# Prompt attention: score groups of rows and columns alternate in one run, values follow in two blocks; f32r masks; preparation in the sample stage

## What is computed

```python
q_r = rope(q, fpos)                       # 16 heads of 64, 4 groups of keys and values
k_s, v_s = rope(kv[:, :, 2], fpos), kv[:, :, 3]
k_w, v_w = rope(kv[:, :, 4], fpos), kv[:, :, 5]
s_c = einsum('bqgrd,bngd->bqgrn', q_b, ck) * scale      # compressed blocks
p_c = masked_softmax(s_c, (c_end[None, :] <= qp[:, None])[None, :, None, None, :])
o_c = einsum('bqgrn,bngd->bqgrd', p_c, cv)
p_s = masked_softmax(s_s, m_s)            # selected branch; o_s = p_s v_s
p_w = masked_softmax(s_w, m_w)            # window branch;   o_w = p_w v_w
return g_b[..., 0:1] * o_c + g_b[..., 1:2] * o_s + g_b[..., 2:3] * o_w
```

## Time and profile before

| | |
|---|---|
| median of 3 runs | 2354.88 us (2352.86 to 2372.43) |
| profiled execution | 2356.08 us, its span 2354.3 us |
| mean granted clock of TensorE | 0.838 |
| busy: PE, DVE, ACT, POOL | 2059.4, 924.4, 610.2, 133.2 us (87, 39, 26, 6% of the span) |

### The profile page before, as it was taken

How to read it: one execution, slowest core, us unless ns; L and a number is a source line. 1 busy time by engine, 2 the same in 40 slices (tenths; PEclk the granted TensorE clock), 3 DMA queues, 4 the chain that set the end, 5 groups by cost and what they waited for, 6 DMA issues and landing times.

```text
span 2354.3 us, 33541 instructions
## 1 busy us (share of the span) xinstructions
PE 2059.4 (87%) x13375; PEld 1838.6 (78%) x13375; DVE 924.4 (39%) x1372; ACT 610.2 (26%) x847; POOL 133.2 (6%) x171
## 2 busy tenths in 40 slices
PE   3999676999999696997687779999998699999968
PEld 3777375999999696996574447777788699999958
DVE  4687745433334644114011122322333634343363
ACT  4222144322312223221101111222123423232223
POOL 0000003000000000004000021011100200000000
PEclk8999797999999898996666655555589799999979
DMA  4211013322222121213221200000003122222211
GB/s 131 59 36 36 18 54 118 97 83 89 89 89 89 36 77 53 72 54 92 55 62 46 72 0 1 1 1 1 1 1 99 36 90 87 91 82 79 89 36 56
DMA packets 149763, 138.82 MB, mean 59 GB/s; under 512 B 22674, under 2 KB 146914, under 8 KB 149471
## 3 DMA queue, kind: packets, MB, share of 16 engines
q1 hardware_dynamic: 148175, 129.94, 17.8%
q0 software_dynamic: 1504, 7.74, 1.0%
HBM read 130.79 MB, written 10.87 MB: 60 GB/s over the span
## 4 chain that ended last, share of the span: by engine, by line
PE 82%; DVE 9%; issue 2%; ACT 2%; SPq 1%; POOL 1%; DMA 0%; ACTq 0%; DVEq 0%; POOLq 0%
PE ps L360 47%; PE ps L1209 5%; PE ps L439 3%; PE ps L1182 3%; PE ps L399 3%; PE ps L1180 2%; PE ps L1196 2%; PE ps L1194 2%; PE ps L913 1%; DVE sub_out L1899 1%; PE ps L1052 1%; PE ps L739 1%; PE ps L738 1%; PE ps L740 1%; DVE rstd L466 1%
## 5 line engine op out<-in xcount | busy, mean ns | idle before, releaser
L360 PE MATMUL ps<-x_hi,w_hi 128*128 128x272 f32 x1920 | 409.4, 295 | 75.7 <-DVE x_lo L481 33.9
L360 PE MATMUL ps<-x_hi,w_lo 128*128 128x272 f32 x1920 | 404.1, 293 | 0.0
L360 PE MATMUL ps<-x_lo,w_hi 128*128 128x272 f32 x1920 | 403.2, 292 | 0.0
L360 PEld LDWEIGHTS ps<-x_hi,w_hi 128*128 128x128 f32 x1920 | 308.4, 193 | 84.4 <-issue 47.8
L345 DVE TENSOR_TENSOR w_lo<-w_raw,w_hi 128x2048 fp32r<-128x2048 f32 x102 | 233.6, 2293 | 250.1 <-ACT w_hi L340 249.1
L360 PEld LDWEIGHTS ps<-x_lo,w_hi 128*128 128x128 f32 x1920 | 309.3, 193 | 0.0
L360 PEld LDWEIGHTS ps<-x_hi,w_lo 128*128 128x128 f32 x1920 | 307.0, 193 | 0.0
L340 ACT ACTIVATE w_hi<-w_raw 128x2048 fp32r<-128x2048 f32 x102 | 194.5, 1907 | 296.5 <-PE ps L360 287.6
L360 PE MATMUL ps<-hid_hi,w_lo 128*128 128x272 f32 x1024 | 212.0, 288 | 0.0
L360 PE MATMUL ps<-hid_hi,w_hi 128*128 128x272 f32 x1024 | 211.6, 288 | 0.0
L360 PE MATMUL ps<-hid_lo,w_hi 128*128 128x272 f32 x1024 | 211.1, 288 | 0.0
(11 more groups left out here) (339 smaller groups left out, 2838.9 us busy)
## 6 DMA issues: line engine op xcount, KB each, us to landing
w_raw<-in_ffn_w_in SPq DMA_DIRECT2D x64, 512.0 KB, 4.6
w_raw<-in_ffn_w_out SPq DMA_DIRECT2D x64, 512.0 KB, 4.3
w_raw<-in_nsa_w_in SPq DMA_DIRECT2D x20, 512.0 KB, 4.3
w_raw<-in_conv_w_in SPq DMA_DIRECT2D x16, 512.0 KB, 5.5
w_raw<-in_ple_w_gate SPq DMA_DIRECT2D x16, 512.0 KB, 4.2
w_raw<-in_conv_w_out SPq DMA_DIRECT2D x8, 512.0 KB, 4.4
w_raw<-in_nsa_w_o SPq DMA_DIRECT2D x8, 512.0 KB, 4.6
x_tok<-in_x_prompt SPq DMA_DIRECT2D x4, 512.0 KB, 8.1
```

The costliest lines, as they stand in the source:

```text
L360: m = pe.matmul(o_, w[par][:, wcols:wcols + P], x[:, k, c_], start=f, stop=l)
```

## The change

- TensorE's order: in step i (now -1 to 15) the row groups of head i+1 and the column groups of head i alternate, j by j, in one run. Then come `out_rows` and the compressed parts, the ten values of head i for the selected branch, `shift(i+1)`, `cmp_out`, and the ten values of head i for the window branch. Values thus belong to head i and no longer to head i-1, and pT has one buffer instead of two. ScalarE and VectorE follow the new order.
- In each tile the low multiply comes second and the mask last. The mask is made of f32r copies of identity and mask (IDR, CAUR).
- The row form's low multiply takes 68 partitions instead of 64; GpSimd sets QB's four to zero ahead of each head's row scores.
- The preparation for the first group and the first two queries is moved into the sample stage: ScalarE's ahead of its sample work, GpSimd's (`prompt_prep`) behind it. v_one and the two f32r masks lie over a part of kv_tok, so GpSimd waits for the stores of kv_tok ahead of them.

The diff, cut to its core:

```diff
-        (PT,), e = over(xt_at, ("pT", [P, 2, 5, SEQ], F32))
+        (PT,), e = over(xt_at, ("pT", [P, 5, SEQ], F32))
...
+        (VX, IDR, CAUR), e = over(kv_at, ("v_one", [P, 2, 2, QT, HD + 1], F32), ("ident_r", [P, P], F32R),
+                                  ("causal_r", [P, P], F32R))
...
+        def keys_high(act, L, g):
+            if g >= 2:
+                act.wait_ge(S["t_full"], 5 * GQ * (g - 1))
+            for br in range(2):
+                L(act.activation(KA[g % 2][0:HD, br, :], KT[:, br, g, :], ACT.Copy), S["k_hi"], wait=False)
+
+        def q_high(act, L, i):
+            if i >= 3:
+                act.wait_ge(S["t_full"], 5 * (i - 2))
+            rows = slice(i % 2 * HD, i % 2 * HD + HD)
+            L(act.activation(QA[i % 3][rows, :], QR[rows, i // 2, 0:SEQ], ACT.Copy), S["q_hi"], wait=False)
+
         def samp_act(act, L):
+            keys_high(act, L, 0)
+            for i in range(2):
+                q_high(act, L, i)
...
+                if f == 0:
+                    pe.wait_ge(S["mask_r"], 1)
...
-                    pe.matmul(out[:, qt * P:n], IDB[:, :], CAUB[:, :], start=False, stop=False)
-                    m = pe.matmul(out, qb[0:HD, qs], KB[g % 2][0:HD, br, 0:n], start=False, stop=True)
+                    pe.matmul(out, qb[0:HD + 4, qs], KB[g % 2][0:HD + 4, br, 0:n], start=False, stop=False)
+                    m = pe.matmul(out[:, qt * P:n], IDR[:, :], CAUR[:, :], start=False, stop=True)
...
-                    pe.matmul(out[:, 0:P], CAUB[:, :], IDB[:, :], start=False, stop=False)
-                    m = pe.matmul(out, KB[g % 2][0:HD + 4, br, ks], qb[0:HD + 4, kt * P:SEQ], start=False, stop=True)
+                    pe.matmul(out, KB[g % 2][0:HD + 4, br, ks], qb[0:HD + 4, kt * P:SEQ], start=False, stop=False)
+                    m = pe.matmul(out[:, 0:P], CAUR[:, :], IDR[:, :], start=False, stop=True)
...
-            def values(i, br, j):
+            def values(i, br):
...
                 for j in range(5):
                     if i + 1 < NHD:
                         score_rows(i + 1, j)
-                    if i >= 1:
-                        values(i - 1, 0, j)
+                    if i >= 0:
+                        score_cols(i, j)
+                if i % 2 == 0 and i >= 2:
+                    out_rows(i // 2 - 1)
                 if (i + 1) % GQ == 0 and i + 1 < NHD:
                     cmp_scores((i + 1) // GQ)
-                if i % GQ == 0 and 0 <= i < NHD:
+                if i % GQ == 0:
                     cmp_probs(i // GQ)
-                for j in range(5):
-                    if 0 <= i < NHD:
-                        score_cols(i, j)
-                    if i >= 1:
-                        values(i - 1, 1, j)
-                    if j == 2 and i + 1 < NHD:
-                        shift(i + 1)
-                if i % GQ == 0 and 0 <= i < NHD:
+                if i >= 0:
+                    values(i, 0)
+                if i + 1 < NHD:
+                    shift(i + 1)
+                if i % GQ == 0:
                     cmp_out(i // GQ)
-                if i % 2 and i >= 3:
-                    out_rows((i - 3) // 2)
+                if i >= 0:
+                    values(i, 1)
...
-                if i >= 2 and j == 0:
-                    act.wait_ge(S["b_full"], i - 1)
-                L(act.activation(PT[:, i % 2, j, :], PS[:, 2 + (5 * i + j) % 2, :], ACT.Exp), S["t_exp"], wait=False)
+                if i and j == 0:
+                    act.wait_ge(S["b_full"], i)
+                L(act.activation(PT[:, j, :], PS[:, 2 + (5 * i + j) % 2, :], ACT.Exp), S["t_exp"], wait=False)
...
             for i in STEPS:
                 if i % GQ == 2 and i + 2 < NHD:
-                    keys_high(i // GQ + 1)
-                if i + 2 < NHD:
-                    q_high(i + 2)
-                if i % GQ == 0 and 0 <= i < NHD:
+                    keys_high(act, L, i // GQ + 1)
+                if 2 <= i + 2 < NHD:
+                    q_high(act, L, i + 2)
+                for j in range(5):
+                    if i >= 0:
+                        exps(i, j)
+                if i % 2 == 0 and i >= 2:
+                    out_rows(i // 2 - 1)
+                if i % GQ == 0:
                     cmp_probs(i // GQ)
-                for j in range(5):
-                    if 0 <= i < NHD:
-                        exps(i, j)
-                    if j == 2 and i + 1 < NHD:
-                        shift_rows(i + 1)
+                if i + 1 < NHD:
+                    shift_rows(i + 1)
+                if i % GQ == 0:
+                    cmp_out(i // GQ)
                 if (i + 1) % GQ == 0 and i + 1 < NHD:
                     cmp_exp((i + 1) // GQ)
-                if i % GQ == 0 and 0 <= i < NHD:
-                    cmp_out(i // GQ)
-                if i % 2 and i >= 3:
-                    out_rows((i - 3) // 2)
             out_rows(NHD // 2 - 1)
 
         def prompt_dve(dve, L):
...
-                if i >= 2:
-                    combine_win(i - 2)
-                if i % GQ == 0 and 0 <= i < NHD:
-                    cmp_norm(i // GQ)
+                if i >= 1:
+                    combine_win(i - 1)
                 if i + 1 < NHD:
                     for j in range(5):
                         maxima(i + 1, j)
                     shift(i + 1)
                 if (i + 1) % GQ == 0 and i + 1 < NHD:
                     cmp_max((i + 1) // GQ)
-                if i >= 1:
-                    combine_sel(i - 1)
+                if i >= 0:
+                    combine_sel(i)
+                if (i + 1) % GQ == 0 and i + 1 < NHD:
+                    cmp_norm((i + 1) // GQ)
             combine_win(NHD - 1)
 
-        def prompt_pool(pool, L):
-
...
+            L(pool.memset(QB[i % 3][HD:HD + 4, :].bitcast(F32), 0.0))
...
-            keys(0)
-            queries(0)
-            cmp_vals(0)
-            vals(0)
+            keys(pool, L, 0)
+            queries(pool, L, 0)
+            queries(pool, L, 1)
+            cmp_vals(pool, L, 0)
+            pool.wait_ge(stores, 16 * N_KV_ST)
+            L(pool.memset(VX[:, :, :, :, HD:HD + 1], 1.0))
+            vals(pool, L, 0)
+            L(pool.tensor_copy(IDR[:, :], ID))
+            L(pool.tensor_copy(CAUR[:, :], CST[:, C_CAU:C_CAU + P]))
+            pool.drain().then_inc(S["mask_r"], 1)
+
+        def prompt_pool(pool, L):
...
             samp_pool(pool, L)
+            prompt_prep(pool, L)
```

More of the change, by code:

```diff
@@ L1138, in trunk @@
         V_ORDER = [(qt, kt) for qt in range(QT) for kt in range(qt + 1)]
-        STEPS = range(-1, NHD + 1)
+        STEPS = range(-1, NHD)
         def bank_uses():
@@ new lines, in keys, with queries @@
+        def keys(pool, L, g):
+            for br in range(2):
+                pool.wait_ge(S["k_hi"], 2 * g + br + 1)
+                L(pool.tensor_tensor(KA[g % 2][HD:P, br, :], KT[:, br, g, :], KA[g % 2][0:HD, br, :].bitcast(F32), ALU.subtract),
+                  S["k_prep"])
+                L(pool.tensor_copy(KB[g % 2][0:HD, br, :], KA[g % 2][0:HD, br, :].bitcast(F32)), S["k_prep"])
+        def queries(pool, L, i):
+            rows = slice(i % 2 * HD, i % 2 * HD + HD)
+            pool.wait_ge(S["q_hi"], i + 1)
+            other = slice((i + 1) % 2 * HD, (i + 1) % 2 * HD + HD)
+            hi = QA[i % 3][rows, :].bitcast(F32)
+            L(pool.memset(QB[i % 3][HD:HD + 4, :].bitcast(F32), 0.0))
+            L(pool.tensor_copy(QA[i % 3][other, :], hi), S["q_prep"])
+            L(pool.tensor_tensor(QB[i % 3][0:HD, :], QR[rows, i // 2, 0:SEQ], hi, ALU.subtract), S["q_prep"])
```

92 lines of the change are left out of this document (33 added, 59 removed).

## The result

The changed kernel takes 2208.9 us (median; 2203.4 to 2244.0), the kernel before beside it 2355.1 us; the ratio is 0.9346, with a 95% interval of 0.9299 to 0.9394. The forecast was 2196 us. The profiled execution took 2204.82 us, against 2197.2 in my sum. So the time came out nearly as worked out. The experiments show that a good part of the reasons behind it did not.

The account below looks back on a forecast made before the run. The prediction took TensorE, at one of two clock speeds, as the prompt stage's bound; its terms summed to 247.1 us instead of 406.0, giving 2197.2 us profiled and 2196 median. The 8-in-10 range was 2165 to 2325.

Parts of the forecast that it names:

- The opening: Start of the prompt stage: moving its preparation into the sample stage was to gain 12.4 us at cost 0.
- The cover: Sample stage: ScalarE's moved copies run while TensorE waits for GpSimd's q_bd work; without that, a cost of 2.5 us.
- Row form: Row scores on 68 partitions priced like column scores: 6.6 us instead of 10.0, 3.4 less per head at 1.2 GHz.
- the row form saves nothing: Rival on row scores: 68 partitions as dear as 64, 37 us more, 2235, within the forecast's range; no chance of its own.
- the clock term: Prompt stage: step 0's cmp_out raises TensorE's clock to 2.4 GHz and it stays, giving 15 heads x 12.3 us.
- the half in which it fell is gone: Argument for a lasting clock: it fell in a row-score half of the 64-partition form with values between, which the change removes.
- Masks: f32r masks in the score groups: visible weight loads were to cost 0.8 us a head at 1.2 GHz, 0.4 at 2.4.
- the large term: Prompt stage: granted clock 1.00 from about 1400 us to the stage's end, with that end near 1610.
- A head: One head of the prompt stage after the change: 23.5 us at 1.2 GHz, 12.3 at 2.4 GHz.
- The new waits: TensorE waits 0.8 us for a ScalarE copy ahead of cmp_out in four groups and of cmp_probs in three.
- and it stays: Prompt stage: once raised by step 0's cmp_out, the clock was to remain at 2.4 GHz.
- the other engines fit in 12.3: Per head at 2.4 GHz, VectorE's maxima (2.9 us) and ScalarE's exponentials (3.0) were to fit in 12.3 us.

Follow-up runs that it names:

- e3_order_only: The changed kernel with the old multiplies back (64 partitions, bf16 masks in the middle of a group), keeping the new order and moved preparation: 2309.8 us.
- e1_rows64: The changed kernel with only the row groups' low product back on 64 partitions, without the memset: 2401.5 us, ten executions between 2315 and 2406.
- e2_bf_masks: The changed kernel with bf16 masks instead of f32r ones, in the same last place of each group: 2213.8 us.
- e9_old_order: The changed kernel with the old order on all four engines, keeping the new multiplies and moved preparation: 2209.1 us.
- e4_forms_only: The kernel before with only the new multiplies (68 partitions for rows, f32r masks last), in its old order and with its old preparation: 2218.2 us.
- e7_small_cmp_out: The changed kernel with the first group's cmp_out cut from 4 x 256 to 4 x 32 columns: 2247.6 us.
- e6_prep_back: The changed kernel with the preparation back at the opening of the prompt stage, on ScalarE and GpSimd: 2232.3 us.

## Why the prediction was right, and where it wasn't

**The opening, 12.4 us: right.** The first score multiply followed the last transpose of the sample stage (1362.26) by 2.65 us. In the kernel before this distance was 15.1 us:

```profile
1359.37 0.48 PE L1057 MATMUL ps<-consts,o_s 128*128 128x128 f32 x1 [0.37 <-ACT o_s L1074]
```

15.11 - 2.65 is 12.5, forecast 12.4. The cover held: in the changed kernel ScalarE's copies lie beside GpSimd's q_bd work, TensorE's wait for that work is 3.93 us in both kernels (up to 1230.60 before and 1232.66 after), and GpSimd is done with everything at 1251 us.

```profile
1226.78 1.15 ACT L1068 ACTIVATE k_hi_lo<-k_T 64x512 fp32r<-64x512 f32 x2 [1.64 <-DVEq L337]
...
1230.32 2.29 POOL L1135 COPY q_bd_rot<-qT_rot 64x64 f32<-64x64 f32 x8
```

**Row form, 3.4 us a head: the size roughly right, its place in the argument wrong.** Row groups cost what column groups do: head 0's five take 6.5 us (1364.91 to 1371.37, where cmp_scores begins), against 6.6 forecast. The warm loss was near too: a head of `e3_order_only` takes 14.4 us at 2.4 GHz, against 12.08. But the rival "the row form saves nothing" was priced as 37 us, as if the clock didn't depend on it. It would have cost 101 us (`e3_order_only`) or about 190 (`e1_rows64`). The step that failed in the clock term is "the half in which it fell is gone": I took the halves' order for the cause, because values stood between the row groups there. That half also had the 64-partition products, named in the same sentence, and these were the cause.

**Masks: nothing, forecast 0.4 us a head at 2.4 GHz.** A bf16 mask does take less by itself: 0.04 us from start to start (`e2_bf_masks`, 1405.76 to 1405.80), an f32r one 0.06 (1401.89 to 1401.95). But the main product behind it then takes 0.32 us instead of 0.28 for 512 columns, and the head as a whole 12.12 us (1405.21 to 1417.33) instead of 12.08. So the term of 0.4 (0.8 at 1.2 GHz) should have been nothing, and `e2_bf_masks` had no 7 us to gain. That it is not faster but 5 us slower goes with its 68 us at 1.2 GHz, where the changed kernel spent 51 (its stage is 7.8 us longer).

**Order: nothing by itself** (`e9_old_order`), where nearly the whole large term rested on it. That the number came out right is luck: the change has the form beside the order, and the form alone (`e4_forms_only`) would have brought 137 of the 146 us.

**A head.** At 2.4 GHz 12.08 us (1458.22 to 1470.30), forecast 12.3; at 1.2 GHz 22.1 (`e7_small_cmp_out`, 1401.27 to 1423.35), forecast 23.5.

**The new waits: right**, 3.1 us in four and 2.1 in three.

**The clock: right in the rise, wrong in "and it stays".** Cutting cmp_out takes the rise of 1399.2 us away, so it is that one's cause; but a full cmp_out didn't always bring it (`e6_prep_back`). The fall at 1501.6 us was not foreseen; 20.5 us at 1.2 GHz cost 20.5 x (1 - 12.1 / 22.1) = 9.3 us. Its cause is another step that failed: "the other engines fit in 12.3". I compared VectorE's maxima and ScalarE's exponentials with a head's mean. What counts is the chain ahead of one bank: in every fourth step cmp_norm and combine_win stand before the maxima, and TensorE waits 1.8 us. The waits for the maxima are 7.0 us in all, 1.2 of them in step 0.

**The sum.** From the first score multiply to the first transpose of the last out_rows the stage took 250.7 us, forecast 247.1. The opening run took 0.5 us less. Step 0 was 3.6 us cheaper (25.1 for 28.7): 1.4 by the cheaper head at 1.2 GHz and 2.0 by its last ten values, which ran at 2.4. What came behind it was 7.8 more (214.3 from 1401.35 to 1615.61, forecast 206.5). The fall (9.3) and the maxima's waits (5.8) would make that 15.1. Two terms of the forecast were too high and hid half of it: the heads were 0.2 us cheaper each, some 3 in all, and the last head has no row scores beside it and no shift, which the 15 x 12.3 overlooked. It took 8.6 us, from its column scores at 1605.51 to the end of its twenty values at 1614.06.

The other 4 us of the profiled 7.6 lie outside the stage, 2.9 of them ahead of it: the same transpose stands at 1362.26 instead of 1359.37. Of these, 2.1 were there ahead of the sample stage and of the moved copies (a multiply at 1224.73 before stands at 1226.80 after), and 0.8 arose in its first part, next to a wait that grew from 3.8 to 5.2 us; what lengthened it isn't shown. The median lies 4 us above the profiled execution.

## What to carry to other kernels

Where TensorE is busy and slow, compare start-to-start times of multiplies of equal columns: a product on 64 partitions between ones on 128 took 0.3 us more in itself and 0.3 around it at 1.2 GHz, and padding it with zero rows cost TensorE nothing and GpSimd a memset of four rows a head. A busy share near 100% hid that, and the clock was down for most of the stage. Whether a load begins ahead of its multiply or only with it shows the same. Then look at what the other engines do just ahead of the bank that TensorE waits for, not at their share of a step: one wait of 1.8 us in three cost a further 9 us of half clock. And undo each part of a change alone before saying which one worked; here an order that took most of the edit gave nothing beside a change of two lines.
